# Eight unread products in the first stage of a two-layer decoder step

## The chip, the cores and the metric

The kernel runs on one core of one Trainium2 chip. Its time is the device time of one execution in microseconds (us); several executions are timed, and their median counts. One execution was also taken by the hardware profiler, and all rows below come from that one. A core has five engines that run side by side, each with its own list of instructions: TensorE (PE in the rows, its weight loads PEld), VectorE (DVE), ScalarE (ACT), GpSimd (POOL) and SyncE (SP, which here only starts transfers). They meet at semaphores. Sixteen DMA engines move data between memory and the core. TensorE's clock is granted at one of two levels, 1.2 or 2.4 GHz; a row shows the granted clock as a share, 0.50 or 1.00.

## The reference

What is computed is one inference step of two layers over 320 tokens: 256 of one new sequence and 8 of each of eight running sequences. Each sub-layer normalises x, then scales and shifts it by rows that come from a conditioning vector c. Cut to what the first stage needs:

```python
mod = (jax.nn.silu(c) @ a_w + a_b).reshape(B, N_SUB, 3, D_MODEL)[:, :, :, None, :]

def rms_norm(x, g):
    y = xf * lax.rsqrt(jnp.mean(xf * xf, axis=-1, keepdims=True) + RMS_EPS)
    return (y * g.astype(F32)).astype(x.dtype)

def modulate(y, i):
    return rms_norm(y, g_pre[i]) * (1.0 + mod[:, i, 1]) + mod[:, i, 0]

x = residual(x, swiglu(modulate(x, 0), f_in[0], f_out[0]), 0, FFN_RES_WEIGHT)
mix, ... = mixer(modulate(x, 1), ...)
x = residual(x, mix, 1, 1.0)
x = residual(x, swiglu(modulate(x, 2), f_in[1], f_out[1]), 2, FFN_RES_WEIGHT)
```

The model dimension is 1024 (eight tiles of 128), the hidden one of SwiGLU 2816.

## The kernel before

x lies with the model dimension on the partitions, as `x[128, 8, 320]`. A large product is made in three parts (`mm3`, lines 520 to 525): the weights are split by ScalarE into a high part WHI (`hi_split`, in the first stage `hi_part`) and by VectorE into a low part WLO (`lo_split`, `lo_part`), the activations into hmh and hml, and high by high, high by low and low by high are added up in PSUM.

The whole kernel is written out by hand: each engine's list stands in the order of the code, and `wait_ge` on a semaphore is where one engine waits for another. The first stage is everything up to the end of the first iteration of the first SwiGLU. On TensorE it stands in this order:

1. Squares of x (line 926): ScalarE squares two tiles of x at a time as they land, TensorE sums them over partitions with a matrix of ones. The eight tiles go to four column groups of one PSUM bank, bank 5.
2. ScalarE copies the four partial sums (line 1255), and a product with ones (line 929) adds them up. From its result ScalarE makes the factor rst of the norm.
3. For each tile k of the eight: `conditioned(k)`, eight products of silu(c) with one megabyte of conditioning weights (line 953), which wait for the transfer of that tile; ScalarE copies the result (`first_copy`, line 1268); `column(k)` turns it so that it stands on the partitions (two products of 9 columns, line 961). VectorE and ScalarE then scale and shift tile k and split it into hmh and hml.
4. `started(0, k)` and `started(1, k)` multiply tile k with the first two weight tiles (six products of lines 523 to 525 each).

`conditioned(k + 2)` stands ahead of `started(0, k)` in the loop, so conditioning runs two tiles ahead. SyncE starts the eight conditioning tiles (line 396) and the first weights in parts (line 400), then the weights of the next iteration (line 392), once the low halves of the old ones are made, and two pieces of conditioning weights of the next sub-layer (line 386). Those two pieces are multiplied on TensorE (`partial(0)`, `partial(1)`, line 535) as the first thing behind the first stage; then the SwiGLU iterations follow.

Products of float32 operands are shown as two records each, those of the split operands as one.

Of the kernel before, what the change touches and what calls it, by code (L numbers as in the profile page):

```python
# [161 lines left out]
def trunk(nc, A, O):  # L162

    ctx = ExitStack()
    with ctx:
        def sb(name, shape, dt=F32):
            return ctx.enter_context(nc.sbuf_tensor(name, shape, dt))
# [13 lines left out]
        cst = sb("cst", [P, NC_])  # L181
# [29 lines left out]
        PS = ctx.enter_context(nc.psum_tensor("PS", [P, 8, 512], F32))  # L211
# [34 lines left out]
        ones = cst[:, C_ONE:C_ONE + P]  # L246
# [270 lines left out]
        def _(pe):  # L517
            mm = nc.tensor.matmul
# [399 lines left out]
                        mm3(PS[:, t, 0:T], 0, k * 256 + t * P, hmh[:, k, :], hml[:, k, :], k == 4, False)  # L918


            pe.wait_ge(s_c, 1)
            pe.wait_ge(s_cst, 16)
            for k in range(KT):
                pe.wait_ge(s_sqx, k + 1)
                j = k % 4
                last = mm(PS[32 * j:32 * j + 32, 5, 0:T], ones[:, 0:32], sq[:, k, :], start=(k < 4), stop=(k >= 4))
            last.then_inc(s_xg, 1)
            pe.wait_ge(s_xc, 1)
            mm(PS[:, 5, 0:T], ones, rt[:], start=True, stop=True).then_inc(s_xst, 1)

            def started(slot, k):

                i = FIRST_USE.get((slot, k))
                if i is not None and i < len(s_part0):
                    pe.wait_ge(s_whi, i + 1)
                    pe.wait_ge(s_wlo, i + 1)
                elif i is not None:
                    split_ready(slot, 0)
                for t in (0, 1):
                    last = mm3(PS[:, 2 * slot + t, 0:T], slot, k * 256 + t * P, hmh[:, k, :], hml[:, k, :],  # L940
                               k == 0, k == KT - 1)
                if k == KT - 1:
                    last.then_inc(s_used[slot], 1)

            def conditioned(k):

                pe.wait_ge(s_first[k], 16)
                if k > 1:
                    pe.wait_ge(s_m0, k - 1)
                for i in (0, 1):  # L950
                    for j in range(4):
                        kt = 2 * j + i
                        last = mm(PS[32 * j:32 * j + 32, 6 + k % 2, 0:256], cT[:, kt, :],  # L953
                                  first[k][:, kt * 256:(kt + 1) * 256], start=(i == 0), stop=(i == 1))
                last.then_inc(s_p0, 1)

            def column(k):

                pe.wait_ge(s_a0, k + 1)
                for i in (0, 1):  # L960
                    last = mm(PS[:, 6 + k % 2, 256 + NS * i:256 + NS * (i + 1)], adps[k % 2][:, i * P:(i + 1) * P], sel,
                              start=True, stop=True)
                last.then_inc(s_t0, 1)

            conditioned(0)
            column(0)
            conditioned(1)
            column(1)
            for k in range(KT):
                if 0 < k < KT - 2:  # L970
                    conditioned(k + 2)
                pe.wait_ge(s_hml, k + 1)
                started(0, k)
                if k == 0:
                    conditioned(2)
                if k + 2 < KT:
                    column(k + 2)
                if k % 2:
                    started(1, k // 2)
# [1077 lines left out]
```

## Time and profile before

| | |
|---|---|
| time, median of 3 executions | 1369.86 us (1366.56 to 1371.04) |
| profiled execution, own time | 1369.65 us |
| its span, first to last instruction | 1367.9 us |
| busy share of the span: PE, PEld, DVE, ACT, POOL | 97%, 90%, 50%, 39%, 6% |
| mean granted clock of TensorE | 0.994 |
| bytes moved, mean rate | 255.43 MB, 187 GB/s |

The span runs from the first to the last instruction of the program; 1.75 us of the execution's own time lie outside it. A matmul's end is modelled, so a busy TensorE is not one at its peak. Where the profile has no record of the clock, it prints 1.00.

### The profile page before, as it was taken

To read this page: it belongs to the slowest core of one execution; us is meant where nothing else is said; L and a number is where in the kernel's file an instruction comes from. 1 tells how busy PE (TensorE), PEld (TensorE's weight loads), DVE (VectorE), ACT (ScalarE), POOL (GpSimd) and SP (SyncE) were. 2 spreads that over 40 slices of the span, in tenths; PEclk is the share of its full clock that TensorE was granted. 3 is DMA by queue.
4 is the path that set the end of the run, shared out by engine and by line. 5 is a ranking of instruction groups with operands and counts; after the bars stand their busy time and mean duration, and the time that the engine had idled before them with its cause. 6 is when DMAs were issued, how large, how long until landed. Compare 5 with 4: busy or idle time off the path is not lost.

```text
span 1367.9 us, 23311 instructions
## 1 busy us (share of the span) xinstructions
PE 1333.2 (97%) x10152; PEld 1235.2 (90%) x10152; DVE 683.5 (50%) x740; ACT 539.0 (39%) x643; POOL 85.0 (6%) x103
## 2 busy tenths in 40 slices
PE   7999999999989999999999999999998999999997
PEld 4888999979969699999979999998897779999996
DVE  4533434357865634444364344434777664444443
ACT  5423333343544533333343333333343554333331
POOL 0000000000360000000000000000017100000000
PEclk8999999999999999999999999999999999999998
DMA  9876556374326644446375544645531473444531
GB/s 359 309 261 263 203 195 257 126 280 159 121 96 261 223 154 145 146 161 262 128 265 212 188 137 144 250 179 216 208 146 65 160 263 124 152 147 138 197 134 39
DMA packets 50628, 255.43 MB, mean 187 GB/s; under 512 B 6254, under 2 KB 11246, under 8 KB 30702
## 3 DMA queue, kind: packets, MB, share of 16 engines
q1 hardware_dynamic: 49790, 251.77, 50.5%
q8 instruction: 68, 1.11, 0.3%
q10 hardware_dynamic: 576, 1.31, 0.3%
q0 software_dynamic: 176, 1.09, 0.2%
q14 instruction: 18, 0.15, 0.0%
HBM read 249.26 MB, written 4.89 MB: 186 GB/s over the span
## 4 chain that ended last, share of the span: by engine, by line
PE 94%; DVE 2%; DMA 2%; ACT 1%; issue 1%; SPq 0%; ACTq 0%; DVEq 0%
PE PS L523 28%; PE PS L525 27%; PE PS L524 27%; PE PS L535 3%; PE PS L587 1%; DMA stage<-in_ada_w 1%; PE PS L724 1%; PE PS L953 1%; PE PS L743 1%; PE PS L766 0%; DMA x<-in_x 0%; PE PS L689 0%; DVE raw L1706 0%; PE PS L595 0%; PE PS L871 0%
## 5 line engine op out<-in xcount | busy, mean ns | idle before, releaser
L523 PE MATMUL PS<-hmh,WHI 128*128 128x320 f32 x1856 | 577.3, 311 | 4.2 <-DVE hml L1397 3.6
L524 PE MATMUL PS<-hml,WHI 128*128 128x320 f32 x1856 | 571.6, 308 | 0.0
L525 PE MATMUL PS<-hmh,WLO 128*128 128x320 f32 x1856 | 571.6, 308 | 0.0
L1354 DVE TENSOR_TENSOR WLO<-raw,WHI 128x2048 fp32r<-128x2048 f32 (+1 forms) x146 | 361.0, 2472 | 397.3 <-ACT WHI L1050 397.3
L1050 ACT ACTIVATE WHI<-raw 128x2048 fp32r<-128x2048 f32 (+1 forms) x146 | 300.1, 2056 | 358.9 <-PE PS L525 352.6
L523 PEld LDWEIGHTS PS<-hmh,WHI 128*128 128x128 f32 x1856 | 348.4, 188 | 27.4 <-issue 25.3
L524 PEld LDWEIGHTS PS<-hml,WHI 128*128 128x128 f32 x1856 | 348.6, 188 | 0.3
L525 PEld LDWEIGHTS PS<-hmh,WLO 128*128 128x128 f32 x1856 | 348.4, 188 | 0.0
L523 PE MATMUL PS<-hhl,WHI 128*128 128x320 f32 x704 | 216.6, 308 | 0.0
L524 PE MATMUL PS<-hhl,WHI 128*128 128x320 f32 x704 | 216.5, 308 | 0.0
L525 PE MATMUL PS<-hhl,WLO 128*128 128x320 f32 x704 | 216.5, 308 | 0.0
L524 PEld LDWEIGHTS PS<-hhl,WHI 128*128 128x128 f32 x704 | 131.9, 187 | 0.0
L523 PEld LDWEIGHTS PS<-hhl,WHI 128*128 128x128 f32 x704 | 131.9, 187 | 0.0
L525 PEld LDWEIGHTS PS<-hhl,WLO 128*128 128x128 f32 x704 | 131.9, 187 | 0.0
L1140 ACT ACTIVATE y<-PS 128x640 f32<-128x640 f32 x44 | 30.9, 703 | 177.6 <-PE PS L525 177.6
L1536 DVE TENSOR_TENSOR y<-y,PS 128x640 f32<-128x640 f32 x44 | 36.1, 821 | 103.9 <-PE PS L525 103.5
L1119 ACT ACTIVATE sq<-PS 128x640 f32<-128x640 f32 x18 | 12.7, 705 | 112.5 <-PE PS L525 112.5
L1524 DVE TENSOR_TENSOR acc<-acc,sq 128x320 f32<-128x320 f32 x18 | 8.9, 494 | 71.7 <-ACT sq L1119 64.2
L535 PE MATMUL PS<-stage,cT 128*32 128x512 f32 x336 | 40.6, 597 | 2.0 <-DMA stage<-in_ada_w 2.0
L1542 DVE TENSOR_TENSOR hhl<-y,hhl 128x640 fp32r<-128x640 f32 x44 | 36.0, 818 | 0.0
L1507 DVE TENSOR_TENSOR y<-y,rst 128x640 f32<-128x640 f32 (+1 forms) x30 | 20.1, 686 | 30.9 <-ACT rst L1069 30.9
L1863 POOL TENSOR_TENSOR y<-y,modC 128x128 f32<-128x128 f32 x8 | 3.3, 408 | 492.8 <-ACT y L1128 492.8
(256 smaller groups left out, 850.7 us busy)
## 6 DMA issues: line engine op xcount, KB each, us to landing
raw<-in_w_in SPq DMA_DIRECT2D x86, 1024.0 KB, 4.8
raw<-in_w_out SPq DMA_DIRECT2D x32, 1408.0 KB, 6.0
stage<-in_ada_w SPq DMA_DIRECT2D x84, 512.0 KB, 7.0
ada<-in_ada_w SPq DMA_DIRECT2D x44, 512.0 KB, 6.9
raw<-in_m_in SPq DMA_DIRECT2D x20, 1024.0 KB, 4.8
raw<-in_m_out SPq DMA_DIRECT2D x8, 1024.0 KB, 4.8
z<-in_ada SPq DMA_DIRECT2D x3, 1024.0 KB, 10.5
big<-in_ada SPq DMA_DIRECT2D x2, 1024.0 KB, 15.8
```

What stands on the lines that cost most here:

```text
L523: mm(out, hi, rhi, start=first, stop=False)
L524: mm(out, hi, rlo, start=False, stop=False)
L525: return mm(out, lo, rhi, start=False, stop=last)
L535: last = mm(PS[32 * j:32 * j + 32, 6 + c % 2, :], cT[:, k, :], halves[j // 2][:, (j % 2) * 512:(j % 2) * 512 + 512], start=(k == 0), stop= ...
L587: last = mm(PS[:, 5, 0:T], ones, sq[:, k, :], start=(k == 0), stop=(k == KT - 1))
L724: last = mm(PS[p0:p0 + 64, bank + e, i * CH:(i + 1) * CH], left, right, start=True, stop=True)
L1050: a_(WHI[:, slot, 0:width], raw[:, slot, 0:width], ACT.Copy).then_inc(s_hi[slot], 1)
L1140: a_(sg, PS[:, 0:2, 0:T], ACT.Silu).then_inc(s_gread, 1)
L1354: tt(WLO[:, slot, 0:width], raw[:, slot, 0:width], WHI[:, slot, 0:width].bitcast(F32), ALU.subtract).then_inc(s_lo[slot], 1)
L1507: done[i] = ch.mark(tt(y[:, a:b, :], y[:, a:b, :], rst2[:].unsqueeze(1).to_broadcast([P, b - a, T]), ALU.mult))
L1536: tt(hf, sg, PS[:, 2:4, 0:T], ALU.mult).then_inc(s_uread, 1)
L1542: tt(hl[:, it * 2:it * 2 + 2, :], hf, hh[:, it * 2:it * 2 + 2, :].bitcast(F32), ALU.subtract).then_inc(s_hl, 1)
```

## The change

A function `unread(width)` issues one product of the matrix of ones with the first columns of the constants, into PSUM bank 4, which nothing reads in this stage and which no semaphore follows. It is called eight times on TensorE: with 320 columns behind the squares of tiles 1, 3 and 5, with 448 behind all squares, with 256 behind `conditioned(0)`, with 384 behind `column(0)`, with 256 behind `conditioned(1)` and with 256 behind `conditioned(2)`. No other engine's list changes; on TensorE no other instruction is removed or moved against another.

```diff
+            def unread(width):
+
+                mm(PS[:, 4, 0:width], ones, cst[:, 0:width], start=True, stop=True)
+
             pe.wait_ge(s_c, 1)
             pe.wait_ge(s_cst, 16)
             for k in range(KT):
                 pe.wait_ge(s_sqx, k + 1)
                 j = k % 4
                 last = mm(PS[32 * j:32 * j + 32, 5, 0:T], ones[:, 0:32], sq[:, k, :], start=(k < 4), stop=(k >= 4))
+                if k in (1, 3, 5):
+                    unread(320)
             last.then_inc(s_xg, 1)
+            unread(448)
             pe.wait_ge(s_xc, 1)
             mm(PS[:, 5, 0:T], ones, rt[:], start=True, stop=True).then_inc(s_xst, 1)
...
             conditioned(0)
+            unread(256)
             column(0)
+            unread(384)
             conditioned(1)
+            unread(256)
             column(1)
             for k in range(KT):
                 if 0 < k < KT - 2:
@@ -973,6 +983,7 @@
                 started(0, k)
                 if k == 0:
                     conditioned(2)
+                    unread(256)
```

The list of TensorE at its start, before the change (line, product, number of equal ones; sq are the squares, cst holds the ones, z the first conditioning tiles):

```order
L926 MATMUL PS<-sq,cst 32x320 x8
L929 MATMUL PS<-rt,cst 128x320
L953 MATMUL PS<-z,cT 32x256 x8
L961 MATMUL PS<-cst,adp 128x9 x2
L953 MATMUL PS<-z,cT 32x256 x8
L961 MATMUL PS<-cst,y 128x9 x2
```

The same place in the changed kernel, whose lines are numbered four higher at the squares and seven higher behind them (960 is `conditioned`, 968 `column`):

```order
L930 MATMUL PS<-sq,cst 32x320 x2
L923 MATMUL PS<-cst 128x320
L930 MATMUL PS<-sq,cst 32x320 x2
L923 MATMUL PS<-cst 128x320
L930 MATMUL PS<-sq,cst 32x320 x2
L923 MATMUL PS<-cst 128x320
L930 MATMUL PS<-sq,cst 32x320 x2
L923 MATMUL PS<-cst 128x448
L936 MATMUL PS<-rt,cst 128x320
L960 MATMUL PS<-z,cT 32x256 x8
L923 MATMUL PS<-cst 128x256
L968 MATMUL PS<-cst,adp 128x9 x2
```

Each pair of squares but the last now has an unread product between it and the next pair, and one of 448 columns stands ahead of the product that waits for ScalarE's copy.

Further on, around the third conditioning tile, before the change (z is its conditioning tile, big the next one):

```order
L525 MATMUL PS<-hmh,WLO 128x320
L953 MATMUL PS<-z,cT 32x256 x8
L961 MATMUL PS<-cst,adp 128x9 x2
L953 MATMUL PS<-big,cT 32x256 x8
L523 MATMUL PS<-hmh,WHI 128x320
```

And in the changed kernel:

```order
L525 MATMUL PS<-hmh,WLO 128x320
L960 MATMUL PS<-z,cT 32x256 x8
L923 MATMUL PS<-cst 128x256
L968 MATMUL PS<-cst,adp 128x9 x2
L960 MATMUL PS<-big,cT 32x256 x8
```

An unread product of 256 columns stands where TensorE waited for ScalarE's copy; from the fourth tile on the list is as it was.

## Rows read from the trace of the kernel before

**Rows 1.** The profile's page: busy time of TensorE; its granted clock in 40 slices.

```profile
PE 1333.2 (97%) x10152; PEld 1235.2 (90%) x10152; DVE 683.5 (50%) x740; ACT 539.0 (39%) x643; POOL 85.0 (6%) x103
...
PEclk8999999999999999999999999999999999999998
```

**Rows 2.** Stretches: busy PE, PEld, DVE, ACT, POOL; granted clock, DMA share, GB/s.

```profile
5.60:8.80 3.20, 3.20 (x14) 0.64 (x16) 0.49 (x3) 2.14 (x4) 0.00 (x0) 1.00 1.09 412
...
12.40:15.70 3.30, 1.68 (x20) 0.94 (x20) 2.72 (x11) 2.16 (x5) 0.00 (x0) 1.00 1.00 400
...
15.80:25.90 10.10, 9.51 (x54) 6.55 (x55) 4.77 (x15) 3.98 (x9) 0.00 (x0) 0.50 1.02 419
26.00:35.76 9.76, 9.76 (x94) 7.32 (x93) 6.63 (x21) 5.79 (x12) 0.00 (x0) 1.00 0.69 280
35.76:45.95 10.19, 9.85 (x74) 8.75 (x74) 6.39 (x14) 7.15 (x9) 0.38 (x1) 1.00 0.79 288
45.95:48.85 2.90, 2.30 (x19) 0.36 (x17) 1.07 (x2) 0.00 (x0) 0.87 (x2) 1.00 1.04 437
48.85:100.00 51.15, 51.15 (x357) 47.90 (x354) 20.92 (x14) 17.68 (x14) 0.00 (x0) 1.00 0.77 289
```

**Rows 3.** Timeline of TensorE: start, duration (us), line, product, idle time before it.

```profile
10.48 0.81 PE L929 MATMUL PS<-rt,cst 128*128 128x320 f32 x2 [0.96 <-ACT rt L1255]
11.21 1.07 PE L953 MATMUL PS<-z,cT 128*32 128x256 f32 x16
12.79 0.61 PE L961 MATMUL PS<-cst,adp 128*128 128x9 f32 x4 [0.50 <-ACT adp L1268]
14.31 1.07 PE L953 MATMUL PS<-z,cT 128*32 128x256 f32 x16 [0.92 <-DMA z<-in_ada]
15.89 1.02 PE L961 MATMUL PS<-cst,y 128*128 128x9 f32 x4 [0.50 <-ACT y L1268]
...
18.64 1.94 PE L953 MATMUL PS<-z,cT 128*32 128x256 f32 x16
...
35.76 1.07 PE L953 MATMUL PS<-stage,cT 128*32 128x256 f32 x16
```

**Rows 4.** Line 926, duration min/median/max (ns), from 7.4 to 8.7 and from 8.9.

```profile
L926 PE MATMUL PS<-sq,cst x6: 740/741/741, 6.7 to 8.0; 128*32 128x320 f32 x6
...
L926 PE MATMUL PS<-sq,cst x4: 433/471/513, 8.7 to 9.1; 128*32 128x320 f32 x4
```

**Rows 5.** Timeline of ScalarE: copy of line 1255, second copy of line 1268.

```profile
9.99 0.44 ACT L1255 ACTIVATE rt<-PS 128x320 f32<-128x320 f32 x1
...
15.45 0.38 ACT L1268 ACTIVATE y<-PS 128x256 f32<-128x256 f32 x1
```

**Rows 6.** SyncE's issues of two tiles (timeline), and their time to landing (DMA issues).

```profile
7.23 0.43 SPq L396 DMA_DIRECT2D y<-in_ada  x1
...
y<-in_ada SPq DMA_DIRECT2D x1, 1024.0 KB, 19.9
...
11.22 3.67 SPq L396 DMA_DIRECT2D stage<-in_ada  x1
...
stage<-in_ada SPq DMA_DIRECT2D x1, 1024.0 KB, 22.2
```

**Rows 7.** Timelines of VectorE and SyncE behind the sixth tile: low half, next weights.

```profile
35.40 0.69 DVE L1473 TENSOR_TENSOR WLO<-raw,WHI 128x512 fp32r<-128x512 f32 x1 [0.39 <-ACT WHI L1274]
...
36.18 0.33 SPq L392 DMA_DIRECT2D raw<-in_w_in  x1
```

**Rows 8.** Chain of waits from 36 to 49 us: start, duration, what.

```profile
35.83 1.04 PE PS L953 x16
36.87 0.83 SPq L386
...
38.70 9.12 DMA stage<-in_ada_w
...
47.85 1.07 PE PS L535 x8
```

## The prediction

> **What bounds the kernel now.** I read the page first. TensorE is busy 97% of the span, and its granted clock is full in every slice but the first and the last [rows 1]. So the first 34 us are the only place where the clock could give anything to a busy TensorE.
>
> The view by stretches shows where. From 15.8 to 25.9 us the granted clock is 0.50, the 1.2 GHz level, and TensorE is busy 9.51 of 10.10 us; before it the stretch from 12.4 to 15.7 had TensorE busy 1.68 of 3.30 us, and behind it the clock is at 2.4 GHz with TensorE busy without a break [rows 2]. The reader is to see that TensorE is the bound where it is slow.
>
> TensorE's timeline shows what that costs and what precedes it. The same eight conditioning products take 1.07 us at 11.21 and 14.31 and 1.94 us at 18.64; ahead of the fall stand waits of 0.96, 0.50, 0.92 and 0.50 us, on ScalarE three times and on a transfer once [rows 3].
>
> Nor is the very start at the full clock, although the stretch from 5.60 to 8.80 prints 1.00 [rows 2]: one pass of squares lasts 741 ns up to 8.7 us and down to 433 ns right after, which is the ratio of the two levels with some fixed time on top [rows 4]. I take the start up to about 8.9 us as 1.2 GHz.
>
> Behind TensorE stand three things that it cannot outrun. ScalarE copies the sums of the squares at 9.99 and the second conditioned tile at 15.45 [rows 5]. The conditioning tiles land when they land: the sixth (y) at 7.23 + 19.9 = 27.1, the eighth (stage) at 11.22 + 22.2 = 33.4 [rows 6]. And the next weights are requested at 36.18, when VectorE has made a low half begun at 35.40 [rows 7]; two pieces of conditioning weights follow, and the chain of waits at the stage's end goes from the eighth tile's products (35.83) over SyncE's issues (36.87) and a transfer (9.12 us) to the products at 47.85 [rows 8]. From 48.85 on TensorE is busy 51.15 of 51.15 us [rows 2], so what the stage gains or loses reaches the end.
>
> **The change, part by part.** Nothing is removed or moved, eight float32 products are added.
>
> *Price of one.* The nearest row is line 929, the same shape with 320 columns: two passes from 10.48, the next product starting at 11.21, so 0.73 us [rows 3]. That has an isolated product's start in it. From below: 741 less 433 ns is what half of a pass's streaming costs, 0.31 us, so a pass streams 0.3 us at 2.4 GHz and 0.6 at 1.2, a product 0.6 and 1.2 us [rows 4]. Among busy neighbours I take the lower: 0.6 us for 320 columns, 0.48 for 256, 0.72 for 384, 0.84 for 448, twice that at the low level.
>
> *The first four, at the squares.* They stand in front of work that is awaited. From 5.60 the list up to the signal to ScalarE is four pairs of squares and three unread products, seven times 1.2 us at the low level. If the clock rises at 8.9 as it does now, 3.3 us make 2.75 of the seven, and 4.25 × 0.6 = 2.55 us more end them at 11.45. ScalarE would take the copy at 9.99 [rows 5], so it is 1.5 us late; the product of 448 columns ends at 12.3, and line 929 starts there and not at 10.48: 1.8 us late. Bounds: with the full clock from the first square the last pair starts at 8.7 [rows 4], squares and unread product end at 8.7 + 0.6 + 0.84 = 10.1, and the cost is nothing; without any rise the squares end at 5.6 + 8.4 = 14.0, the unread product at 15.7, and it is 5.2 us. I take 1.8, because the row shows the rise with less work in front of it than the changed kernel has.
>
> *The other four.* Two of 256 columns (0.48 us) lie in the waits of 0.50 us ahead of line 961, the one of 384 (0.72) in the wait of 0.92 us for a transfer [rows 3]; with everything 1.8 us later that transfer has landed, but then ScalarE's second copy, which also moves from 15.45 by 1.8, is what is waited for. The third of 256 stands in the like wait behind the third tile. Each costs nothing at the full clock. Without that cover, or at the low level, one of 256 columns costs 0.5 us beyond its wait.
>
> *What the clock gives.* TensorE's stretches are fuller in the changed kernel: between 12.4 and 15.7 three of the additions put 1.7 us of work into what held 1.68 in 3.30 us [rows 2]. I expect the clock to stay at 2.4 GHz once it has risen. Then the 9.51 us of the low stretch shrink as its conditioning products do, by 1 − 1.07/1.94 = 45%, or 4.3 us. Less the 1.8 us of the start, TensorE would be 2.5 us ahead at 26 us.
>
> *What is late next.* The eighth conditioning tile. TensorE starts it at 35.76 and it lands at 33.4, so it cannot be more than 2.3 us ahead [rows 3, 6]. (For the sixth the room is larger.) Since 2.5 exceeds 2.3, the landing sets it, and the size of the start's delay does not matter up to 2.0 us; each microsecond beyond that comes off the gain.
>
> *Behind that.* All that follows the eighth tile on TensorE is unchanged, 10.19 us up to 45.95 [rows 2]. The weights' request at 36.18 and the two pieces hang on tiles six to eight and move by as much; the DMA engines stand at 0.69 and 0.79 of their time from 26 to 45.95 [rows 2], so earlier requests are served earlier. The wait that ends at 47.85 moves too, and so does all from 48.85.
>
> **Sum.** −2.3 us against the profiled execution's own 1369.65 gives 1367.35. That execution lies 0.2 us below the median of the runs, so I set 1367.4 and change nothing else. A measurement of this kernel can tell about 0.3%, or 4.1 us, from no change; this gain is 0.17%.
>
> **A record and durations at odds.** The printed clock of the start and the squares' durations disagree [rows 2, 4]. The Trainium skill (TensorE: Matmul & The Clock Gate, Seeing it yourself) warns that the clock's events in a profile can't be fully trusted. By the print the start's delay would be nothing and TensorE 4.3 us ahead; by the durations it is 1.8 and 2.5. The landing allows 2.3 in both, so the sum stays.
>
> **The rivals.**
>
> *Slower: the clock falls all the same.* The additions are short, and by the end of the second tile TensorE still stands still between copies. Then the low stretch remains, the start's 1.8 us are not earned back, and the third 256-column product costs 0.5 us more at the low level: 1369.65 + 2.3 = 1371.9. It decides if the granted clock is 0.50 again somewhere from 15 to 26 us; if moreover the rise comes late, up to 5.7 us are lost. Against it speaks that the present fall follows a stretch of half-empty time and that this is what is filled. The Trainium skill (TensorE: Matmul & The Clock Gate, Why this matters for your kernels) names long idle gaps between bursts of products as what throttles; by that rule none of the gaps here would do, the change would have nothing to act on, and the time would be this rival's. The trace speaks against the rule: the clock fell behind gaps of under one microsecond [rows 2, 3].
>
> *No gain: the transfer at the stage's end does not move.* The pieces are awaited at 47.85 already, and in the last stretch the DMA engines are full (1.04) [rows 2, 8]. If the requests are served no earlier, TensorE waits 2.3 us longer there and the time is 1369.7. Against it: the engines have room just before.
>
> *More: the profiled execution is a mild one of before.* The shown runs spread over 4.5 us. If in others the low stretch begins earlier or lasts longer, the median holds more than the profile shows; two more microseconds would make −4.3 and 1365.5. The profile neither supports nor excludes it, except that its own time is close to the median.
>
> **How the numbers follow.** Forecast 0.70, clock falls 0.12, no gain 0.10, more 0.08. The time is the forecast's, 1367.4. The range runs from the case of more (1365.5) to no gain with the scatter of a median (1370.4); it leaves out the slower rival and a little at the bottom. Slower by over 0.3% needs that rival and a late rise, 0.03; faster by over 0.3% needs nearly all of the case of more, 0.07; within 0.3% is the rest, 0.90.
>
> **What the changed profile would show.** Right: granted clock 1.00 from some 9 us to the end, conditioning products of 1.07 us throughout, line 929 one to two microseconds late, the eighth conditioning tile starting close to 33.4 and waiting for its transfer, the products of line 535 that now start at 47.85 near 45.5. Wrong: a stretch at 0.50 behind 12 us; an eighth tile later than 34.5, which would mean that the copies or the start's delay bound the stage; or pieces that still land at 47.8.

## The result, and the profile after

The change made the kernel slower: median 1378.02 us over 20 executions against 1371.01 over 20 of before, ratio 1.0054 with an interval of [1.0036, 1.0071]. The executions also spread more, 1368.49 to 1388.37 against 1366.56 to 1375.47. The profiled one took 1375.92, its span is 1374.1 us, 6.2 more than before.

In the profiled execution the first stage did gain, but the time was lost a thousand microseconds later. The profile's page after the change (instructions of the span, granted clock in 40 slices):

```profile
span 1374.1 us, 23343 instructions
...
PEclk9999999999999999999999999999998899999998
```

The 8 of the first slice [rows 1] has become a 9, and two slices near 1055 us have become an 8. The span has 32 instructions more: each of the eight float32 products is two weight loads and two matmuls. The view by stretches of the changed kernel (columns as in [rows 2]):

```profile
11.20:35.25 24.05, 23.69 (x205) 14.75 (x201) 15.69 (x54) 13.32 (x29) 0.00 (x0) 1.00 0.91 369
...
1050.82:1053.86 3.04, 1.30 (x57) 1.09 (x57) 1.73 (x3) 1.96 (x8) 3.04 (x4) 1.00 0.05 19
1055.60:1076.10 20.50, 20.50 (x150) 11.67 (x148) 9.76 (x19) 6.48 (x23) 5.05 (x4) 0.50 0.28 103
```

The low stretch of [rows 2] from 15.8 to 25.9 is gone, and one of 20.5 us stands in the second layer's mixer, where TensorE is busy 20.50 of 20.50 us. TensorE's timeline at the start, after the change:

```profile
6.89 1.44 PE L923 MATMUL PS<-cst 128*128 128x320 f32 x2
...
9.47 1.44 PE L923 MATMUL PS<-cst 128*128 128x320 f32 x2
...
11.62 0.81 PE L923 MATMUL PS<-cst 128*128 128x320 f32 x2
...
13.02 1.02 PE L923 MATMUL PS<-cst 128*128 128x448 f32 x2
13.87 0.70 PE L936 MATMUL PS<-rt,cst 128*128 128x320 f32 x2
14.50 1.07 PE L960 MATMUL PS<-z,cT 128*32 128x256 f32 x16
15.50 0.70 PE L923 MATMUL PS<-cst 128*128 128x256 f32 x2
16.08 0.61 PE L968 MATMUL PS<-cst,adp 128*128 128x9 f32 x4
...
35.25 1.07 PE L960 MATMUL PS<-stage,cT 128*32 128x256 f32 x16
...
46.59 1.04 PE L535 MATMUL PS<-stage,cT 128*32 128x512 f32 x8
```

Two unread products of the start take 1.44 us and the third 0.81: the clock rose later than in the kernel before, and line 936 (929 before) starts at 13.87, not 10.48 [rows 3]. The conditioning products take 1.07 us throughout. The eighth tile starts 0.5 us early, the products that started at 47.85 [rows 8] start at 46.59.

Then the second mixer, before the change (TensorE's timeline; line 743 is `levels`, 56 products of 64 columns for a full group):

```profile
1038.14 0.85 PE L683 MATMUL PS<-cst,z 128*128 128x128 f32 x6 [1.01 <-issue]
...
1045.45 0.64 PE L743 MATMUL PS<-sq 64*64 64x64 f32 x30
1047.72 0.68 PE L743 MATMUL PS<-sq 64*64 64x64 f32 x26 [1.63 <-issue]
...
1054.37 1.04 PE L743 MATMUL PS<-raw,sq 64*64 64x64 f32 x56
1055.34 1.16 PE L795 MATMUL PS<-sq 64*128 64x128 f32 x14
1056.82 0.49 PE L795 MATMUL PS<-sq 64*128 64x128 f32 x2 [0.33 <-issue]
...
1059.81 1.93 PE L814 MATMUL PS<-big,sq 64*64 64x512 f32 x8
...
1070.11 0.61 PE L868 MATMUL PS<-sq,big 64*64 64x256 f32 x2 [0.26 <-ACT sq L1217]
```

with the full clock throughout (stretches, columns as in [rows 2]):

```profile
1038.14:1054.37 16.23, 14.11 (x523) 11.90 (x523) 10.50 (x24) 5.01 (x12) 15.50 (x21) 1.00 0.19 67
...
1057.10:1075.00 17.90, 17.13 (x196) 10.91 (x196) 13.24 (x23) 10.73 (x35) 6.25 (x5) 1.00 0.33 119
```

and after the change:

```profile
1035.42 0.85 PE L683 MATMUL PS<-cst,z 128*128 128x128 f32 x6 [1.02 <-issue]
...
1042.63 0.41 PE L743 MATMUL PS<-sq 64*64 64x64 f32 x14
1043.95 0.91 PE L743 MATMUL PS<-sq 64*64 64x64 f32 x42 [0.91 <-issue]
...
1050.82 1.04 PE L743 MATMUL PS<-raw,sq 64*64 64x64 f32 x54
1053.61 0.32 PE L743 MATMUL PS<-raw,sq 64*64 64x64 f32 x2 [1.74 <-issue]
1053.86 1.16 PE L795 MATMUL PS<-sq 64*128 64x128 f32 x16
...
1059.03 3.68 PE L814 MATMUL PS<-big,sq 64*64 64x512 f32 x8
...
1076.32 0.64 PE L868 MATMUL PS<-sq,big 64*64 64x256 f32 x2
```

The mixer begins 2.7 us earlier than before. Waits put down to "issue", behind no semaphore, cut groups of products in two. Before, the cut came after 30 of 56 products, now after 14: 16 products earlier, which with their weight loads are 32 instructions, the number added at the start. The next cut that shows stood in line 795 behind 14 products (0.33 us); it now stands behind 54 of 56 products of line 743 and lasts 1.74 us. From 1050.82 to 1053.86 TensorE is thus busy 1.30 of 3.04 us, and 1.7 us later the clock falls: line 814 takes 3.68 us, not 1.93. The second mixer turns 2.7 us of lead into 6.2 of lag (line 868: 1070.11 before, 1076.32 after). The waits themselves are not the loss: those put down to "issue" in lines 743 and 795 add up to 2.4 us before and 3.0 after. Nor does a wait of that length always cost the clock: the 1.63 us of the kernel before did not.

What loads the instructions shows in the DMA views of the changed kernel, the queue kinds with packets, MB and share. From 1041 to 1044 us:

```profile
DMA packets 1, 0.02 MB, mean 5 GB/s; under 512 B 0, under 2 KB 0, under 8 KB 0
## 3 DMA queue, kind: packets, MB, share of 16 engines
q8 instruction: 1, 0.02, 2.0%
```

and from 60 to 360 us, with the stretch beside it:

```profile
q8 instruction: 16, 0.26, 0.3%
...
60.00:360.00 300.00, 299.00 (x2036) 277.38 (x2036) 144.57 (x126) 110.67 (x106) 7.93 (x9) 1.00 0.59 214
```

Over the span there are 68 such packets and 1.11 MB in both kernels, 16 KB each. From 60 to 360 us 16 of them go with 2036 products and 2036 weight loads of TensorE, so one packet with some 255 instructions. That the cuts are waits for such a block is inferred from this and from how they move with the list; the packet at 1041.7 is done 2.2 us before the wait of 0.91 us ends. The Trainium skill (Runtime: NRT & Kernel Launch, Instruction fetch mechanics) says that an engine's instructions are refilled in 16 KiB blocks of 256 and that crossing a boundary is mostly hidden. The blocks agree with these rows. The hiding agrees from 60 to 360 us, where no wait of TensorE is put down to "issue"; among the mixers' small products it doesn't: 0.3 to 1.7 us stand open.

### The profile page after: what moved, and what is told of

It reads as the page before. It is cut to its first block, busy times and chain, and to the rows that moved or that the text cites. A ratio compares the mean times of both kernels' runs of the same rounds, so it can differ in the third digit from the quotient of the medians.

```text
span 1374.1 us, 23343 instructions
## 1 busy us (share of the span) xinstructions
PE 1344.5 (98%) x10168; PEld 1239.9 (90%) x10168; DVE 684.5 (50%) x740; ACT 539.4 (39%) x643; POOL 85.1 (6%) x103
## 3 DMA queue, kind: packets, MB, share of 16 engines
q8 instruction: 68, 1.11, 0.3%
## 4 chain that ended last, share of the span: by engine, by line
PE 95%; DVE 2%; DMA 1%; ACT 1%; issue 1%; SPq 0%; DVEq 0%; ACTq 0%
PE PS L523 28%; PE PS L524 27%; PE PS L525 27%; PE PS L535 4%; PE PS L587 1%; PE PS L724 1%; PE PS L743 1%; DMA stage<-in_ada_w 1%; PE PS L766 1%; PE PS L960 1%; PE PS L923 0%; PE PS L838 0%; PE PS L689 0%; PE PS L595 0%; DMA cst<-in_cst 0%
```

## The experiments

Theory A: the eight products act by their number. They lengthen TensorE's list by 32 instructions, the block boundaries fall elsewhere in the mixers, and a wait among small products costs the clock. A block is taken as 256 instructions. Theory B, the rival: they act by their work (a later or fuller start, another arrival time) and that makes the mixers lose the clock. Each row below has its own kernel before beside it; "clock" is the mean over executions of the granted share; "list" is by how many instructions TensorE's list is longer than before, and where products were added inside the two mixers, from the start to behind the second mixer. With +256 or 0 every mixer instruction stands where it stood before against the blocks.

| run | list | median us | ratio to before | clock |
|---|---|---|---|---|
| changed kernel | +32 | 1378.02 | 1.0054 [1.0036, 1.0071] | 0.9883 |
| eight products of 9 columns | +32 | 1383.88 | 1.0089 [1.0064, 1.0114] | 0.9858 |
| changed, 224 increments | +256 | 1400.77 | 1.0205 [1.0165, 1.0246] | 0.9940 |
| tiles alone, 240 increments | +256 | 1402.14 | 1.0217 [1.0181, 1.0253] | 0.9952 |
| before, 256 increments | +256 | 1404.08 | 1.0231 [1.0195, 1.0266] | 0.9958 |
| changed, 16 products fewer | 0 | 1369.94 | 0.9996 [0.9982, 1.0010] | 0.9945 |
| tiles alone | +16 | 1370.21 | 0.9997 [0.9977, 1.0016] | 0.9948 |
| squares alone | +16 | 1373.70 | 1.0025 [1.0004, 1.0046] | 0.9916 |
| halves | +64 | 1370.89 | 1.0002 [0.9981, 1.0024] | 0.9931 |
| changed, one in the mixer | +32 to +40 | 1371.29 | 0.9994 [0.9978, 1.0009] | 0.9946 |
| tiles, two in the mixer | +16 to +32 | 1370.85 | 0.9998 [0.9981, 1.0015] | 0.9956 |
| changed, four in the mixer | +32 to +64 | 1372.91 | 1.0009 [0.9991, 1.0027] | 0.9954 |
| tiles, one in the mixer | +16 to +24 | 1371.37 | 1.0004 [0.9976, 1.0032] | 0.9936 |

(The kernel before beside these runs had a mean clock of 0.9928 to 0.9938. A clock lower by 0.001 is 2.7 us at half speed, so some 1.4 us of a busy TensorE: the changed kernel's 0.0045 to 0.0055 below it is, as an estimate, 6 to 8 us, as much as the loss.)

**The number without the work.**

```diff
-                    unread(320)
+                    unread(9)
```

(and 9 columns in the other five calls.) 

> All eight unread products stay where they are but have 9 columns each, so TensorE's list is as long as in the changed kernel and the work added is next to nothing. Theory A (place in the list: the instructions of the mixers have moved against the blocks in which TensorE's list is loaded, a wait of some 1.7 us now falls among the mixer's small products, and the clock falls there): the second mixer again has its wait near the end of the small products of line 743, and the times are like the changed kernel's or up to 2 us above, 1374 to 1386 us. Theory B (the fill itself, by the earlier or fuller start, makes the mixers lose the clock): times like the kernel before, 1367 to 1373 us, and no fall in the mixers.

Median 1383.88, every one of 11 executions above 1378. Its second mixer has the same cut, TensorE's timeline:

```profile
1056.79 1.04 PE L743 MATMUL PS<-raw,sq 64*64 64x64 f32 x54
1059.30 0.33 PE L743 MATMUL PS<-raw,sq 64*64 64x64 f32 x2 [1.47 <-issue]
```

and behind it the clock by stretch:

```profile
1061.20:1081.00 19.80, 19.80 (x146) 11.69 (x149) 9.79 (x18) 5.47 (x20) 4.85 (x4) 0.50 0.29 108
```

The products' work isn't needed for the harm. That this run is 5.9 us slower still than the changed kernel is partly its start (its first mixer begins at 375.57, the changed kernel's at 372.52). In its profile the first mixer loses the clock too, which the changed kernel's profile doesn't show (stretch):

```profile
402.60:409.30 6.70, 6.70 (x56) 3.38 (x48) 2.37 (x4) 3.32 (x12) 3.02 (x2) 0.51 0.01 1
```

That fall does not come behind a cut in the list. The last wait ahead of it is 2.18 us for VectorE, in line 827 at 399.70. The profiles of the tiles' products alone, of the halves and of the run with one product in the mixer have a fall of 6.8 us at the same place, from about 399 us, behind 0.53 to 1.25 us of the same wait.

**The work with the list moved by a whole block, and its control.**

```diff
+            for _ in range(224):
+                hold(pe)
             pe.wait_ge(s_c, 1)
```

> The changed kernel with 224 further semaphore increments at the very head of TensorE's list, where it waits for the constants until 5.6 us, so that with the 32 instructions of the eight products the list is longer by 256, one block as it is loaded. Theory A: the mixers wait at the places where the kernel before waits, they keep the clock as often as that does, and what is left is the gain of the first stage: 1367 to 1370 us, 1 to 2 us below the kernel before. Theory B: the mixers lose the clock as in the changed kernel, 1374 to 1386 us.

> Only the four products behind the conditioning tiles, none at the squares, and 240 semaphore increments at the head of TensorE's list, again 256 instructions more in all. Theory A: the mixers as before; without the four products in front of awaited work the start is not late, and if the clock holds the first stage gains up to 2.3 us: 1367 to 1369 us; if it falls in the first stage, as before, 1370 us. Theory B: nothing at the start is fuller before 12 us, half of the harm, 1370 to 1378 us.

> The kernel before with 256 semaphore increments at the head of TensorE's list and no added product: the control for the two aligned runs. Both theories: the increments lie in the 5 us in which TensorE waits for the constants, or end some microseconds behind it; 1369 to 1374 us, with the mixers as before.

All three missed their times by some 30 us: the squares start at 35.35 behind 224 increments, at 37.86 behind 240 and at 40.30 behind 256, so an increment on TensorE takes (40.30 − 35.35) / 32 = 0.155 us, where I had thought that they fit into the first 5 us. The squares in the run with 224 and in the control, and the control's cuts in the second mixer:

```profile
35.35 1.28 PE L932 MATMUL PS<-sq,cst 128*32 128x320 f32 x4 [35.35 <-issue]
...
40.30 2.36 PE L928 MATMUL PS<-sq,cst 128*32 128x320 f32 x16 [40.30 <-issue]
...
1080.73 0.68 PE L743 MATMUL PS<-sq 64*64 64x64 f32 x26 [1.08 <-issue]
...
1089.76 0.48 PE L795 MATMUL PS<-sq 64*128 64x128 f32 x2 [0.22 <-issue]
```

The cuts leave 26 of 56 products of line 743 and 2 of 16 of line 795, as in the kernel before; the other two runs have them there too. Against the control the full fill is 3.3 us faster and the tiles' products alone 1.9, but with 32 and 16 increments fewer their squares start 4.95 and 2.44 us earlier, so from there on they are 1.6 and 0.5 us slower. The mean clock is 0.994 to 0.996, not 0.988: with the list back on its block, neither the fill nor a kernel running 33 us later makes the mixers lose the clock as the changed one does. That speaks against theory B and against the mere hour of arrival. It is not a clean zero: the fill's profile has 6.8 us at half clock in the second mixer, behind line 838, the two others' none. By 40 us the conditioning tiles had landed, so nothing of the start's gain in the changed kernel can be read from these.

**The list back to its length by leaving work out.** In `mm3` the middle product is skipped for the first pair of iteration 1:

```diff
-                mm(out, hi, rlo, start=False, stop=False)
+                if not short[0]:
+                    mm(out, hi, rlo, start=False, stop=False)
```

> The changed kernel with all eight unread products at full width, and 16 products of the first SwiGLU left out (the middle one of three for the first 16 tiles of iteration 1, so a part of the low half of the activations is missing): 32 instructions fewer in TensorE's list, which behind that point is again as long as in the kernel before. The 16 products are worth 16 x 0.147 = 2.35 us. Theory A (place in the list): the mixers wait where the kernel before waits, granted clock 0.991 to 0.998 as there, and the time is the kernel before less 2.35 less the start's gain of 1 to 2: 1366 to 1368 us. Theory B (the fill itself harms the mixers): granted clock 0.982 to 0.990 and 1374 to 1384 us.

The clock came back (0.9945, lowest 0.992, where the changed kernel's highest is 0.995), as theory A has it. Its cuts leave 26 and 2 products again, and its second mixer begins 0.15 us from where the changed kernel's does (1035.42), so the hour of arrival is not what costs the clock (timeline):

```profile
1035.57 0.85 PE L687 MATMUL PS<-cst,z 128*128 128x128 f32 x6 [1.02 <-issue]
...
1044.13 0.68 PE L747 MATMUL PS<-sq 64*64 64x64 f32 x26 [0.81 <-issue]
```

The time, 1369.94, missed A's 1366 to 1368: with the work left out TensorE arrived early and waited until 54.2, when VectorE has made a low half (51.87 + 2.29 us); in the timelines of VectorE and TensorE

```profile
51.87 2.29 DVE L1369 TENSOR_TENSOR WLO<-raw,WHI 128x2048 fp32r<-128x2048 f32 x1 [4.81 <-ACT WHI L1065]
...
54.27 0.38 PE L524 MATMUL PS<-hmh,WHI 128*128 128x320 f32 x1 [1.32 <-issue]
```

so that at most 1.0 of the 2.35 us was earned there.

**Each half of the change alone.** The calls at the squares taken out, and those behind the tiles taken out:

> Only the four unread products behind the conditioning tiles; the list is 16 instructions longer than before, half of the changed kernel's 32. Theory A: the mixers' waits stand 16 instructions off those of before, so their clock is between or of its own kind, but the same as in the run with the squares' products alone, and the two differ by their starts alone, by 1 to 3 us. The start itself: nothing delays line 929; if the clock holds in the first stage the eighth conditioning tile starts 2 us early, if it falls, as before. Theory B: near the kernel before, 1369 to 1372 us, with no falls in the mixers.

> Only the four unread products at the squares; the list is 16 instructions longer than before. Line 929 starts 1.5 to 3 us late, and with the gaps behind the tiles unfilled the clock may fall in the first stage as before: the stage then ends 1 to 3 us later than before. Theory A: the mixers as in the run with the tiles' products alone, times 1 to 3 us above it. Theory B: the full start is what harms the mixers, granted clock 0.982 to 0.990 here and not in the run with the tiles' products alone.

With the tiles' products alone the eighth tile starts at 33.42, just behind its landing (11.01 + 22.2 = 33.2) and without a wait for it, and the products of line 535 start 3.1 us earlier than before. The squares are not late, yet TensorE runs at half speed to about 14 us: line 957 takes 1.94 us at 11.83. TensorE's timeline of that run:

```profile
10.46 1.44 PE L933 MATMUL PS<-rt,cst 128*128 128x320 f32 x2 [0.54 <-ACT rt L1263]
11.83 1.94 PE L957 MATMUL PS<-z,cT 128*32 128x256 f32 x16
...
33.42 1.07 PE L957 MATMUL PS<-stage,cT 128*32 128x256 f32 x16
...
44.74 1.04 PE L535 MATMUL PS<-stage,cT 128*32 128x512 f32 x8
```

The squares' products alone gain nothing: the clock fell within the first stage of the profiled execution, and its first mixer begins at 374.02, where the kernel before begins it at 373.77. Theory A's claim of equal mixers is not cleanly met (clock 0.9948 and 0.9916); a fall in the first stage alone, 6.8 us in that profile, would account for 0.0025 of the 0.0032. But in the profiles it is the tiles' run that loses the clock in both mixers, 6.8 and 3.4 us, and the squares' run in neither. The medians differ by 3.5 us, the starts by 374.02 − 370.65 = 3.4.

**The same work in twice as many products.**

```diff
-                mm(PS[:, 4, 0:width], ones, cst[:, 0:width], start=True, stop=True)
+                for half in (0, 1):
+                    mm(PS[:, 4, 0:width // 2], ones, cst[:, 0:width // 2], start=True, stop=True)
```

> Each unread product of the changed kernel as two of half the width: the same columns, 16 products, the list 64 instructions longer than before. The start as in the changed kernel, up to 1 us later. Theory A: the mixers' waits move on by another 32 instructions and the share of executions that lose the clock there changes, up or down by several us in the median. Theory B: the fill is the same, so are the mixers: 1376 to 1381 us.

Median 1370.89, 7 us below the changed kernel with the same columns. The cuts have moved by another 16 products (timeline):

```profile
1054.82 0.81 PE L743 MATMUL PS<-raw,sq 64*64 64x64 f32 x38
1056.78 0.56 PE L743 MATMUL PS<-raw,sq 64*64 64x64 f32 x18 [1.16 <-issue]
```

38 products ahead of it, where the changed kernel had 54, and 1.16 us instead of 1.74; two of twelve executions still exceed 1378. Its profile keeps the clock in the second mixer behind these cuts and loses it for 6.8 us in the first. This is the plainest case against theory B.

**Work inside the mixer.**

```diff
+                    if n in (4,):
+                        mm(PS[:, 7, :], ones, cst[:, 0:512], start=True, stop=True)
                     levels(n)
```

> The changed kernel with one more unread product per layer, of 512 columns into PSUM bank 7, ahead of the fifth group of small products of line 743 in each mixer: the place where the changed kernel's profile waits 1.74 us and loses the clock. Theory A with the list's loading as the cause of the wait and the half-empty small products as the cause of the fall: the product's 0.9 us lie inside the wait, the wait is that much shorter, the second mixer keeps the clock in more executions, median 1371 to 1375 us, mean granted clock 0.990 to 0.994. If the fall has nothing to do with that place: as the changed kernel or 1 to 2 us above, 1378 to 1380 us, clock 0.988.

> The run with the tiles' products alone, with two such products of 512 columns per layer, ahead of the second and the fifth group of line 743. Theory A: those of its executions that lost the clock in a mixer lose it less often, median 1367.5 to 1369.5 us, 0.996; the products cost at most 0.9 us each where no wait covers them. Otherwise 1370 to 1373 us.

> The changed kernel with four products of 512 columns per layer in the mixers, ahead of the first, second, fourth and fifth group of line 743. Theory A: the mixers keep the clock nearly always, 0.994 or more, and the time is 1367 to 1371 us, the start's gain less what the eight products cost where nothing covers them. If the clock in the mixers does not hang on how full TensorE is there: 1380 us or more.

> The four products behind the conditioning tiles, and one of 512 columns per layer ahead of the second group of line 743, where the run with the tiles' products alone waits 1.20 us in its second mixer. Theory A: the product lies inside that wait and costs nothing, the mixers keep the clock more often, and the start's gain of 3 us is left in more executions: 1368 to 1370 us, 1 to 3 us below the kernel before. If a fall elsewhere in the mixers decides: 1370 to 1372 us, no difference.

With one product the median falls to 1371.29. The profiled execution, the longest of the twelve, loses the clock earlier in the second mixer, behind a wait of 1.40 us in another group (timeline, then stretch):

```profile
1049.35 0.91 PE L743 MATMUL PS<-sq 64*64 64x64 f32 x44 [1.40 <-issue]
```

```profile
1051.00:1064.00 13.00, 13.00 (x208) 9.06 (x210) 5.73 (x11) 2.08 (x8) 9.40 (x10) 0.50 0.23 82
```

It passes the added product at half clock, so it doesn't show what that does to the wait of 1.74 us. More such products keep the clock a little better (0.9954 to 0.9956) and cost about what they keep. Joined with the tiles' products, one or two come out even with the kernel before, 1 to 3 us short of what A led me to expect; four with the whole change miss their 1367 to 1371 by 1.9 us. Since each also moves the list by four instructions, these four runs don't separate the product's work from its place. No version here beats the kernel before beyond its interval.

## Why the prediction was wrong

The step that failed is "From 48.85 on TensorE is busy 51.15 of 51.15 us [rows 2], so what the stage gains or loses reaches the end", with "Nothing is removed or moved" ahead of it. In order of the program nothing is; against the blocks in which the list is loaded, all that follows is. The term that the sum lacked is the clock in the mixers: where 2.3 us faster was forecast, with a chance of 0.03 for slower by over 0.3%, 7.0 us or 0.5% slower was measured. In the profiled execution it is 2.7 + 6.2 = 8.9 us in the second mixer, in the medians 7 us plus the start's gain. Of the 2.7 us of lead 1.25 are the start's (the first mixer begins at 372.52, before at 373.77); the rest was won in the first mixer, where waits put down to "issue" add up to 4.0 us before and 1.8 after, so moved cuts can gain as well. The one profile of before did not show the risk: its 0.994 is the first stage and the end, and the mixers stand at 1.00. Its other executions range down to 0.986, in which stage isn't recorded.

By its own steps:

- *Start late by 1.8 us:* right in kind, mis-sized. Line 936 is 3.4 late. I took the clock's rise at 8.9 us as given; here products at half speed run to about 11, and with the tiles' products alone, with no product added before it, to about 14. It differs from execution to execution.
- *The other four cost nothing at the full clock:* the 256-column ones take 0.58 us (15.50 to 16.08) and the waits of [rows 3] ahead of the turning products are gone. Held.
- *The clock stays at 2.4 GHz:* held in the first stage of the changed kernel, 1.00 from 11.2 to 35.25.
- *The landing of the eighth tile sets the stage, 2.3 us:* it didn't in the changed kernel, since 4.3 less 3.4 leaves 0.9 (0.5 measured), as the text's "each microsecond beyond that comes off the gain" has it. TensorE waits for that landing in the run with the tiles' products and one in the mixer, at 33.51 in its timeline:

```profile
33.51 1.07 PE L959 MATMUL PS<-stage,cT 128*32 128x256 f32 x16 [0.43 <-DMA stage<-in_ada]
```

- *The wait at 47.85 moves too:* to 46.59, by 1.26. The rival of a transfer that doesn't move is out.
- *The slower rival* named a low stretch between 15 and 26 us. The low stretch came, in another stage and for another reason. The case that executions of before differ more than one profile shows was nearer to the matter, but I gave it to the wrong kernel.

Shown are: number and not work does the harm (9 columns, halves), the cuts move with the list's length, and the loss is in the granted clock. That the moved cut is what costs the clock is argued, from the falls that stand some 2 us behind a cut in the second mixer of three profiles (waits of 1.74, 1.47 and 1.40 us). Against it stand waits as long that cost nothing: 1.63 us in the kernel before, 1.47 with the squares' products alone (line 743 at 1047.19). The rule that the prediction weighed, of the Trainium skill (TensorE: Matmul & The Clock Gate, Why this matters for your kernels), that long idle gaps throttle, is not the whole account by these rows: no wait ahead of those falls is longer than 1.74 us. What stays open: why the same cut costs the clock in one execution and not in the next; what share of the recovery in the mixer runs is the product's work; and the first mixer. The changed kernel's one profile keeps the clock there, the run of 9 columns loses it for 6.8 us behind a wait for VectorE, and an execution of the changed kernel at 0.983 has (1 − 0.983) × 2 × 1383 = 47 us at half speed, more than the 20.5 us of the second mixer and some 8 at the end.

## What to carry to other kernels

In an unrolled list like this one, an instruction added early moves every later one of that engine against the blocks in which the list is loaded. Where a later stage issues many small products, look for waits put down to "issue" that cut a group in two, count how far the change moves them, and price the clock that may go with them. Before fitting a gain of a few microseconds, read the granted clock of all executions, not of the profiled one alone.

## What the runs showed of the hardware

A semaphore increment at the head of TensorE's list took 0.155 us. One instruction packet of 16 KB went with some 255 instructions of TensorE. Waits put down to "issue", at places that move with the list's length, reached 1.74 us among products of 64 columns; behind 1.40, 1.47 and 1.74 us of them the clock fell, behind 1.63 us in another execution it did not. One stretch at half clock in the mixer lasted 20.5 us, during which TensorE was busy throughout.
